# First attention of a two-layer block: values stationary and scaled probabilities moving, with the output made transposed in PSUM

## The reference, cut to what matters

```python
o_cmp = jnp.einsum('bghqc,bcgd->bqghd', p_cmp.astype(dt), vc_c)
...
o_slc = jnp.einsum('bghqk,bgqkd->bqghd', p_s.astype(dt), vs_g)
...
o_win = jnp.einsum('bghql,blgd->bqghd', p_w.astype(dt), vwin)
g = lax.dynamic_slice_in_dim(gate_a, q0, Q_BLOCK, axis=1)
o_a = g[..., 0:1] * o_cmp + g[..., 1:2] * o_slc + g[..., 2:3] * o_win
...
p_b = e / (e.sum(axis=-1, keepdims=True) + jnp.exp(sink - m))
o_b = jnp.einsum('bghql,blgd->bqghd', p_b.astype(dt), vbw)
return jnp.concatenate([o_a.reshape(B, Q_BLOCK, NSA_Q_W), o_b.reshape(B, Q_BLOCK, SWA_Q_W)], axis=-1)
```

## Time and profile before

| what | value |
|---|---|
| median of three runs | 3062.44 us (3058.03 to 3063.49) |
| the profiled execution's own time | 3059.4 us |
| its span | 3057.6 us |
| DMA share in the page's slices from 76 to 306 us | 0.3 |
| one weight load of 1 MB, issue to landing (median) | 4.8 us |
| ScalarE busy over the span | 1538.2 us (50%) |
| VectorE busy over the span | 2028.6 us (66%) |

### The profile page before, as it was taken

The page is one execution under the profiler, slowest core; times in us unless marked ns, Lnnn a source line. Parts: engine busy times, 40 slices in busy tenths (PEclk is TensorE's granted clock), DMA queues, the critical chain, the costliest instruction groups (busy, mean ns, idle before and its releaser), DMA issues.

```text
span 3057.6 us, 45171 instructions
## 1 busy us (share of the span) xinstructions
PE 3019.4 (99%) x16816; PEld 2615.9 (86%) x16816; DVE 2028.6 (66%) x2694; ACT 1538.2 (50%) x2134; POOL 20.6 (1%) x42
## 2 busy tenths in 40 slices
PE   9998999999999999999999999999999999999999
PEld 8997898888888888888888888888889888888887
DVE  5566679976888875555555555776566777777443
ACT  4554534555666665444444444544555555555333
POOL 2000000000000000000000000000000000000000
PEclk9999999999999999999999999999999999999999
DMA  7333545565566568766666666444455555555554
GB/s 269 133 132 116 188 159 196 204 228 187 186 239 240 213 219 296 249 240 242 242 241 241 241 241 233 163 147 163 152 179 179 181 195 187 191 180 192 196 189 179
DMA packets 138979, 615.20 MB, mean 201 GB/s; under 512 B 12989, under 2 KB 50062, under 8 KB 73968
## 3 DMA queue, kind: packets, MB, share of 16 engines
q1 hardware_dynamic: 126976, 583.05, 54.0%
q10 hardware_dynamic: 9440, 21.93, 2.0%
q0 software_dynamic: 2464, 8.89, 0.9%
HBM read 578.13 MB, written 36.49 MB: 201 GB/s over the span
## 4 chain that ended last, share of the span: by engine, by line
PE 76%; ACT 6%; DVE 5%; issue 3%; DMA 3%; ACTq 0%; DVEq 0%; SPq 0%
PE bank L642 75%; DMA raw<-in_experts_u_t 3%; ACT high L2275 3%; DVE low L1296 3%; ACT first_both L2520 1%; DVE first L1810 1%; ACT big L2528 1%; ACT big L2499 0%; ACT big L2493 0%; PE bank L912 0%; PE bank L732 0%; DMA raw<-in_w_down_t 0%; DVE resid L1928 0%; DVE big L1722 0%; ACT big L2307 0%
## 5 line engine op out<-in xcount | busy, mean ns | idle before, releaser
L1296 DVE TENSOR_TENSOR low<-raw,high 128x1024 fp32r<-128x1024 f32 x1008 | 1225.4, 1223 | 823.4 <-ACT high L2275 819.0
L2275 ACT ACTIVATE high<-raw 128x1024 fp32r<-128x1024 f32 x1008 | 1055.3, 1057 | 1064.9 <-PE bank L642 733.8
L642 PE MATMUL bank<-act_both,high 128*128 128x512 f32 (+1 forms) x5088 | 1169.2, 358 | 7.3 <-DVE low L1296 3.3
L642 PEld LDWEIGHTS bank<-act_both,high 128*128 128x128 f32 x5088 | 875.8, 190 | 123.5 <-issue 7.5
L642 PE MATMUL bank<-act_both,low 128*128 128x256 f32 x4240 | 713.3, 282 | 0.0
L642 PEld LDWEIGHTS bank<-act_both,low 128*128 128x128 f32 x4240 | 625.9, 191 | 33.1
L642 PE MATMUL bank<-high,weighed_high 128*128 128x512 f32 x1024 | 398.5, 389 | 0.0
L642 PE MATMUL bank<-high,weighed_low 128*128 128x512 f32 x1024 | 398.4, 389 | 0.0
L642 PE MATMUL bank<-low,weighed_high 128*128 128x512 f32 x1024 | 398.3, 389 | 0.0
L642 PE MATMUL bank<-high,act_both 128*128 128x512 f32 (+1 forms) x960 | 310.4, 393 | 3.6 <-DVE act_both L1358 3.6
L642 PEld LDWEIGHTS bank<-high,weighed_high 128*128 128x128 f32 x1024 | 192.3, 188 | 39.8
(11 more groups left out here) (286 smaller groups left out, 1923.1 us busy)
## 6 DMA issues: line engine op xcount, KB each, us to landing
raw<-in_experts_u_t SPq DMA_DIRECT2D x128, 1024.0 KB, 4.9
raw<-in_experts_v_t SPq DMA_DIRECT2D x128, 1024.0 KB, 4.8
raw<-in_w_up_t SPq DMA_DIRECT2D x88, 1024.0 KB, 4.8
raw<-in_w_in_t SPq DMA_DIRECT2D x68, 1024.0 KB, 4.8
raw<-in_w_down_t SPq DMA_DIRECT2D x44, 1024.0 KB, 4.8
raw<-in_w_out_t SPq DMA_DIRECT2D x32, 1024.0 KB, 4.8
raw<-in_peer_wq_t SPq DMA_DIRECT2D x16, 1024.0 KB, 4.8
hidden_dram<-big SPq DMA_DIRECT2D x64, 256.0 KB, 2.9
```

Of the source, the lines that this page charges most:

```text
L642: return pe.matmul(out_, lhs_t, rhs, start=start, stop=stop, skip_group_check=True)
L1296: dve.tensor_tensor(low[b][:, :], raw[r][:, HALF * which:HALF * (which + 1)], as_f32(high[b][:, :]), ALU.subtract).then_inc(low_ready[b], 1)
L2275: act.activation(high[b][:, :], raw[r][:, HALF * which:HALF * (which + 1)], ACT.Copy).then_inc(high_ready[b], 1)
```

## The change

`o1` becomes transposed: 16 chunks of 128 rows (two heads of 64, one from each group) by 256 tokens. In the mix, the values (64 columns) are stationary and the turned probabilities (128 or 256 columns) move; the two units of a pair write partitions 0 to 63 and 64 to 127 of the same bank. The branches of a head are summed in PSUM, so each branch's share, gate over sum, has to be in the probabilities before: VectorE computes it per pair (`shares_of`), and ScalarE multiplies the probabilities by it in four copies (`scale_probs`) before TensorE turns them. ScalarE copies finished banks to `o1` (`copy_chunks`). With `o1` transposed, `turn_o1` and the gain pass go, and the split into high and low parts is done on pairs of chunks. The compressed branch is computed in two parts, with pairs 4 and 20 (scores) and 8 and 24 (turning), and its mixes, now 16 products with 64 stationary columns, follow pairs 12, 14, 28 and 30. The slots change: turning moves from slot s+3 to s+4 and stands ahead of that slot's scores, mixing from s+4 to s+5, the copy of the transposes from s+2 to s+4 on ScalarE, and scaling has ScalarE's slot s+3. Rows of `w_out` are reordered on the host to match. In the diff below, the edits of compressed scores and tables are left out; they keep their amount of work.

```diff
-        o1 = r1.take(TT * D, "p (i d) -> p i d", i=TT)
+        o1_place = r1.take(TT * D)
+        o1 = o1_place.rearrange("p (c t) -> p c t", t=T)
+        attention_squares = o1_place.rearrange("p (i d) -> p i d", i=TT)
...
-        CMP_SCORES_WITH = {NSA_UNITS // 2 + 2 * i: i for i in range(TT)}
-        CMP_PROBS_WITH = {NSA_UNITS - 4 + 2 * g: g for g in range(2)}
+                h=c, swa=swa, g=g, branch=branch, part=part_no, col=SET * (2 * double + g) + j, j=j,
+                round=double - 2 if swa else double // 2))
+        CMP_SCORES_WITH = {4 + 16 * part: part for part in range(2)}
+        CMP_PROBS_WITH = {8 + 16 * part: part for part in range(2)}
...
             def attention_turn(n):
-                pe.wait_ge(probs_ready, 2 * (n + 2))
+                pe.wait_ge(probs_scaled, n + 2)
                 pe.wait_ge(probs_copied, n)
                 for g in range(2):
-                    for k, at in enumerate((0, P, T + 1)):
+                    for k, at in enumerate((T + 1, 0, P)):
                         m = pe.transpose(bank[:, 4 + g, P * k:P * k + P], logits1[:, (n + g) % LOGITS1, at:at + P], ident[:, :])
...
+            def chunk_at(j, g, first=0):
+                return bank[DH * g:DH * g + DH, 6 + j // 2, T * (j % 2) + first:T * (j % 2) + T]
             def attention_mix(n):
+                u = units1[n]
+                j, fresh = u["j"], u["branch"] != 1 and u["j"] % 2 == 0
                 pe.wait_ge(probs_copied, n + 2)
-                for u in units1[n:n + 2]:
-                    pt, o, at = probs_t1[:, u["g"], :], 6 + u["turn"] % 2, u["at"]
-                    if u["first"] and u["turn"] >= 2:
-                        pe.wait_ge(set_read, u["turn"] - 1)
-                    mm(bank[:, o, T + at:T + at + DH], pt[:, 0:P], u["v"][0], stop=False)
-                    mm(bank[:, o, T + at:T + at + DH], pt[:, P:T], u["v"][1], start=False)
-                    mm(bank[:, o, at:at + DH], pt[:, T:T + P], u["v"][0]).then_inc(mixed, 1)
+                if fresh and u["round"]:
+                    pe.wait_ge(chunks_copied, 2 * (u["round"] - 1) + j // 2 + 1)
+                for g in range(2):
+                    mm(chunk_at(j, g, P), units1[n + g]["v"][1], probs_t1[:, g, T:T + P], start=fresh, stop=False)
+                for g in range(2):
+                    m = mm(chunk_at(j, g), units1[n + g]["v"][0], probs_t1[:, g, 0:T], start=False, stop=u["swa"])
+                m.then_inc(mixed, 2)
+                if u["branch"] == 1 and j >= 2:
+                    pe.wait_ge(cmp_copied, u["part"] + 1)
+                    for c in (2 * j - 4, 2 * j - 3):
+                        for g in range(2):
+                            m = mm(chunk_at(c, g), cmp_v[:, SET * g + c, :], cmp_probs_t[:, u["part"], :], start=False)
+                    m.then_inc(chunks_done, 1)
...
+                if slot - 4 in pair_at:
+                    attention_turn(pair_at[slot - 4])
                 if slot in pair_at:
                     attention_scores(pair_at[slot])
-                if slot - 3 in pair_at:
-                    attention_turn(pair_at[slot - 3])
-                if slot - 4 in pair_at:
-                    attention_mix(pair_at[slot - 4])
-                if 43 <= slot < 47:
-                    cmp_mix(slot - 43)
...
+                if slot - 5 in pair_at:
+                    attention_mix(pair_at[slot - 5])
...
-            def turn_o1(half_):
-                for n in range(4):
-                    i, quarter = n // 2, 2 * half_ + n % 2
-                    if n == 0 and half_:
-                        pe.wait_ge(set_read, UNITS // SET + 4)
-                    elif n == 0:
-                        pe.wait_ge(o1_written, 4 + 4)
-                    if n >= 2:
-                        pe.wait_ge(turned_read, TURN0[1] + 4 * half_ + n - 1)
-                    for j in range(4):
-                        c = 4 * quarter + j
-                        m = pe.transpose(bank[:, 4 * half_ + n % 2, P * j:P * j + P], o1[:, i, P * c:P * c + P], ident[:, :])
-                    m.then_inc(turned, 1)
...
-            attention_slot(WOVEN)
-            attention_slot(WOVEN + 1)
-            turn_o1(0)
-            attention_slot(WOVEN + 2)
-            pe.wait_ge(turned_parts, PARTS0[1] + 4)
-            out_group(0, after=lambda k: attention_slot(WOVEN + 3 + k))
+            for slot in range(WOVEN, WOVEN + 3):
+                attention_slot(slot)
+            out_group(0, after=lambda k: attention_slot(WOVEN + 3 + k),
+                      before=lambda p: pe.wait_ge(turned_parts, PARTS0[1] + p + 1))
             pe.wait_ge(logits_ready, 2 * UNITS)
-            out_group(1)
-            turn_o1(1)
+            out_group(1, after=lambda k: attention_slot(WOVEN + 3 + QUAD + k))
             out_group(2)
             out_group(3)
...
+            def split_o1(*pairs_):
+                for n in pairs_:
+                    two = slice(2 * n, 2 * n + 2)
+                    dve.wait_ge(turned_high, PARTS0[1] + n + 1)
+                    dve.tensor_tensor(act_low[:, two, :], o1[:, two, :], as_f32(act_high[:, two, :]), ALU.subtract).then_inc(turned_parts, 1)
...
-            def attention_set(n):
...
+            def shares_of(n):
...
+                heads = slice(u["h"], u["h"] + GROUP_HEADS + 1, GROUP_HEADS)
+                dve.wait_ge(probs_ready, 2 * (n + 2))
+                sums = expsum1.rearrange("p (i n) -> p i n", i=TT)[:, :, u["col"]:u["col"] + SET + 1:SET]
+                m = dve.reciprocal(sums, sums)
+                if not u["swa"]:
                     dve.wait_ge(small_copied, 1)
-                    link(dve.tensor_tensor(sums, sums, gate1[:, :, heads, 1 + branch], ALU.mult))
-                at = N * (g + 2 * (branch == 2)) + DH * SET * part_no
-                part_ = o1[:, :, at:at + DH * SET].rearrange("p i (h d) -> p i h d", d=DH)
-                dst = share1.rearrange("p (i h d) -> p i h d", i=TT, d=DH) if branch == 1 else part_
-                m = dve.tensor_tensor(dst, bank[:, 6 + turn_ % 2, :].rearrange("p (i h d) -> p i h d", i=TT, d=DH),
-                                      row(sums, DH), ALU.mult)
-                m.then_inc(set_read, 1)
-                dve.wait_ge(set_read, turn_ + 1)
-                if branch == 1:
-                    add_o1(part_, dst)
...
+                    link(m)
+                    m = dve.tensor_tensor(sums, sums, gate1[:, :, heads, 1 + u["branch"]], ALU.mult)
+                m.then_inc(shares_ready, 2)
...
             def attention_slot(slot):
-                if slot - 5 in pair_at and units1[pair_at[slot - 5]]["last"]:
-                    for g in range(2):
-                        attention_set(pair_at[slot - 5] + g)
+                if slot - 2 in pair_at:
+                    shares_of(pair_at[slot - 2])
                 if slot in pair_at:
                     attention_logits(pair_at[slot])
-                if slot == 19:
-                    cmp_logits_done()
-                elif slot == 27:
-                    cmp_probs_done()
-                elif 44 <= slot < 48:
-                    cmp_set(slot - 44)
+                if slot % 16 == 5 and slot < 32:
+                    cmp_logits_done(slot // 16)
+                elif slot % 16 == 9 and slot < 32:
+                    cmp_probs_done(slot // 16)
...
+            split_o1(0, 1)
             attention_slot(WOVEN)
+            split_o1(2, 3)
             attention_slot(WOVEN + 1)
-            split_o1(0)
+            split_o1(4, 5)
             attention_slot(WOVEN + 2)
...
+            def scale_probs(n):
+                act.wait_ge(shares_ready, n + 2)
+                for u in units1[n:n + 2]:
+                    at_ = logits1[:, (n + u["g"]) % LOGITS1, :]
+                    for at, width, col in ((0, T, UNITS + u["col"]), (T + 1, P, u["col"])):
+                        m = act.activation(at_[:, at:at + width], at_[:, at:at + width], ACT.Copy, scale=expsum1[:, col:col + 1])
+                m.then_inc(probs_scaled, 2)
...
+            def copy_chunks(n):
+                if n < 4:
+                    act.wait_ge(chunks_done, n + 1)
+                else:
+                    act.wait_ge(mixed, NSA_UNITS + 4 * (n - 3))
+                act.activation(o1[:, 2 * n:2 * n + 2, :].rearrange("p c t -> p (c t)"), bank[:, 6 + n % 2, :], ACT.Copy).then_inc(chunks_copied, 1)
+            chunks_at = {18: 0, 20: 1, 34: 2, 36: 3, 40: 4, 44: 5, 56: 6, 60: 7}
             def attention_slot(slot):
-                if slot - 2 in pair_at:
-                    copy_probs1(pair_at[slot - 2])
+                if slot in chunks_at:
+                    copy_chunks(chunks_at[slot])
+                if slot - 4 in pair_at:
+                    copy_probs1(pair_at[slot - 4])
                 if slot in pair_at:
                     exps1(pair_at[slot])
-                if slot == 25:
-                    act.wait_ge(cmp_shifted, 1)
```

(51 more changed lines are left out.)

141 lines of the change are left out of this document (37 added, 104 removed).

## The result

The changed kernel takes **3089.8 us** (median of 6 runs, 3086.9 to 3092.2), the kernel before 3061.8 on the same chip: ratio 1.0093, 95% interval 1.0080 to 1.0106, so slower. The forecast was 3082 (3068 to 3092). The profiled execution spans 3088.9 us against 3057.6, 31.3 more where the sum said 20.

What follows compares the result with a forecast made beforehand. TensorE bounded the kernel before; the change was to make it wait on a 7.0 us ring. Window terms +20.2, -2.8, -6.6, +11.2, -2.2 sum to about +20: 3079.4, with 3.0 for the median 3082 us, range 3068 to 3092.

Steps and rivals of the forecast that it cites:

- The ring: Woven attention pairs: scores, maxima, exponentials, scaling, turn, next scores form a closed loop of 7.0 us; TensorE stands 1.4 us a pair.
- 0.58 of turning: Last work link of the loop: TensorE's transposes of a pair's probabilities, priced at 0.58 us from the earlier trace.
- the first term: Second pair's scores to pair 38's: 132.4 us against 112.25, +20.2, of which 18 x 7.0 = 126.0.
- the clock falls in the stalls: Rival: TensorE's stops through 18 woven pairs bring it to 1.2 GHz, 75 us more, about 3157; chance 0.03.
- The two compressed score sets: Woven stretch: two compressed score sets on the loop, 36 against 20 instructions, 2.11 us each.
- The group changes: Woven stretch: two changes of product group, where query copies hold TensorE, 0.5 us each.
- sinks and compressed logits: Woven stretch: charged 1.2 us together within the window from second pair's scores to pair 38's.
- Mix: TensorE's mix, eight instructions a pair: 0.96 us, 0.29 less than now; bounds 0.68 side by side, 1.36 one after the other.
- the rival of serial column groups: Rival: column groups run one after the other, mixes cost 1.36 to 1.66, hidden: 3085; counted within the forecast's 0.82.
- To the output product: Input product's end to output product: 4.7 us against 11.29, -6.6, as turn_o1(0), its gains and a 3.63 us wait go.
- Output group 0: 33.9 us against 22.72, +11.2: an 8.7 us stop at pair 40's turn, two loops of 8.0, slow clock 1.4.
- The ring that never binds: Rival: scaling does not stand behind the next exponentials, TensorE stays the bound; about -17 us, 3046; chance 0.09.

Runs made afterwards that it cites:

- run 1: Changed kernel with ScalarE scaling pair s-2 at the head of slot s, before the copy of turned probabilities and the exponentials: 3060.0 us.
- run 2: Changed kernel with three useless scaled copies added on ScalarE ahead of the four real ones of each pair: 3116.5 us.
- run 3: Changed kernel without the four scaling copies of each pair; the turn waits for the exponentials instead: 3050.4 us.
- run 4: Changed kernel with TensorE issuing the scores of pair s before the turn of pair s-4, ScalarE's order unchanged: 3072.7 us.
- run 7: Changed kernel with useless identity transposes on TensorE only in long stops (first turn, group changes, input product's end): 3084.5 us.
- run 6: Changed kernel with twelve useless identity transposes on TensorE ahead of every turn's wait for the scaling: 3092.2 us.
- run 8: Changed kernel with ScalarE's slot ordered copy of pair s-3, scaling of s-2, exponentials of s, and later splits of output chunks: 3049.3 us.
- run 9: Changed kernel with copy, scaling, exponentials in that order, later chunk splits, and two turns moved ahead of the query copies: 3048.0 us.
- run 5: Changed kernel with scaling at the head of ScalarE's slot for pairs 0 to 38 alone, later pairs as changed: 3062.5 us.

## Why the prediction was right, point by point

**The ring** was right in its mechanism and in every link but the turn (scores to maxima 3.11, exponentials 1.77, scaling 1.48), and shown by undoing it (run 1), lengthening it (run 2), taking it away (run 3) and shortening it at another place (run 4). Its prices held too: the 256-wide scaled copy took 494 ns (499 taken), the 128-wide one 388 (391).

**Mis-sized: the turn's link.** "0.58 of turning" came from the earlier trace rows, where the input product follows. In the changed kernel scores follow, and the same six transposes take 0.81. Run 1 has both in one trace: 0.57 ahead of the product, 0.75 ahead of scores. The ring is 7.25 us instead of 7.0, and 18 x 0.25 is 4.5 of the 11.6 us that the first term lacks. The forecast did cite the Trainium skill, TensorEngine Tiling (Array Packing), section Tiling Modes, on the drain at a change of tiling mode, but weighed it for the mix alone; the trace agrees with it here, at 0.18 us.

**Mis-sized: the clock.** The rival "the clock falls in the stalls" was refused for the whole, at +75 us, and rightly: the ring's own stops of 1.5 us leave the granted clock at 1.00 from 128.68 to 157.90. The waits that bring the low clock back each time, of which the Trainium skill tells (TensorE: Matmul & The Clock Gate, section HAM oscillation), are not what these rows show for the ring. The page's waits, put there at some 3 to 5 us, are also longer than the ring's, so "by that rule this would be the outcome" did not follow from it. But the margin was small: with 1 us more on the ring the granted clock of the stretch fell to 0.87 (run 2). And it came true in places, after the stop of 3.5 us at the first turn and after some of the stops of about 2, and the fillers put a price on that: 4.7 us in the woven stretch, of 11.6. The forecast charged a low clock only in the output group.

The other 2.4 us (11.6 - 4.5 - 4.7) lie in run 7's trace as follows. 1.3 is low clock that was left there: behind the stop of 1.87 score groups start 10.33 and 7.98 us apart, where run 6, at full clock, has 9.75 and 7.25. The two compressed score sets cost 0.4 each more than charged (9.75 instead of 7.25 + 2.11), and the first ring takes 7.88, 0.6 more than the others. The group changes come to the 0.5 each that was charged (7.77), and sinks and compressed logits to 0.4 less than charged. So by these traces the clock cost 6.0 us in all, the largest part of the 11.6.

**Mix.** 0.80 us (131.15 to 131.95) instead of 0.96, between the bounds and near the 0.68 of two abreast; the rival of serial column groups (1.36 and up) is out. It lies beside the ring's wait and earned nothing while the ring is closed.

**To the output product,** 5.13 for 4.7: the second scores came at the low clock (1.65 us for 0.92). **Output group 0,** 34.61 for 33.9, right in the sum and different inside. TensorE's timeline there:

```profile
274.71 1.65 PE L645 MATMUL bank<-big 64*128 64x256 f32 x8 [1.29 <-DVE big L1417]
...
287.20 1.54 PE L915 MATMUL bank<-turn_consts,big 128*128 128x128 f32 x6 [5.85 <-ACT big L2286]
...
296.88 0.87 PE L915 MATMUL bank<-turn_consts,big 128*128 128x128 f32 x6 [2.29 <-ACT big L2286]
...
305.85 0.88 PE L915 MATMUL bank<-turn_consts,big 128*128 128x128 f32 x6 [1.68 <-ACT big L2286]
```

Pair 40's turn begins 16.0 us after the input product's end (271.16), as ScalarE's order said (16.2); the stop ahead of it is 5.85, not 8.7, since TensorE had reached it late, at the low clock. In run 7, where fillers kept the clock up, the same stop is 8.63. A low clock ahead of a fixed appointment costs nothing. Behind the stop it was paid: the two rings took 9.7 and 9.0 for 8.0, 2.1 of it turns and scores at the low clock (1.54 for 0.88 and twice 1.6 for 0.92), where the forecast had 1.4 for a clock that comes back slowly; the rest is mostly the turn's link again. The stops at the end of these two rings are 2.29 and 1.68, where the forecast said two near 2.7.

**The ring that never binds,** the rival on the other side, was priced at 3046, some 17 us under the kernel before. Runs 8 and 9 come nearest to that kernel: 3049.3 and 3048.0, 11.6 and 12.9 us under it as timed beside them; run 3, without scaling, is 9.4 under. Up to the input product's end run 9 has the gains as sized (110.29 and 18.43 us, where the rival's terms make 110.45 and 18.88). From there to the end of output group 1 it takes 41.55 us, where they make 37.4: TensorE waits 4.0 us there for ScalarE's copies, which the rival's sum does not have.

**The range** held, with 3089.8 near its upper end, and that is luck in part. The text works out 3070 to 3092 and gives 3068 to 3092; its upper end was made of a dearer scaled copy, a dearer mix, a longer stop at pair 40 and 2 us of clock. The copy, the mix and the stop came out at or under their prices, and the excess came from the turn's link, which had no margin, and from three times the 2 us of clock.

## What to carry to other kernels

A step added between two engines is priced by the loop that it closes, not by the engine's slack: follow one item through every engine's program order until it comes back to where it began, and compare that time with the busiest engine's work per item. If the loop is longer, look first for an order that opens it; here one moved line on ScalarE gave back the whole loss, and further moves turned it into a gain. A stop on TensorE can have a second price, the low clock after it, but only where what follows is not waiting for something else anyway. Look also at what follows a borrowed row: six transposes cost more ahead of scores than ahead of the product that the row had.

## What the runs showed of the hardware

- The same six transposes take 0.57 us ahead of products with 128 stationary rows and 0.75 ahead of products with 64 (run 1; 0.81 after a stop, changed kernel): a change of tile adds about 0.18 us.
- Two column groups of 64 run side by side: the mix's eight instructions (384 moving columns for each group) take 0.80 us, where one group after the other would take 1.36 by the compress products of the earlier trace rows.
- Repeated stops of 1.48 us every 7.25 left the granted clock at 1.00 (128.68 to 157.90); the same ring with nine stops of over 2 us in it ran at 0.87 (run 2). One stop of 3.5 us was followed by 12.6 us at 0.56.
- A stop of about 2 us can go either way. In the changed kernel the stop of 2.15 us before 163.39 is followed by the low clock, the equal one before 226.71 is not, and in run 6 the first of the two is not and the second is:

```profile
163.39 0.51 PE L645 MATMUL bank<-act_both,high 128*128 128x256 f32 x2 [2.15 <-DVE big L1577]
...
165.15 1.48 PE L915 MATMUL bank<-turn_consts,big 128*128 128x128 f32 x6
...
226.71 0.50 PE L645 MATMUL bank<-act_both,high 128*128 128x256 f32 x2 [2.15 <-DVE big L1577]
...
228.24 0.82 PE L915 MATMUL bank<-turn_consts,big 128*128 128x128 f32 x6
```

- Of the fourteen unfilled stops of 2.1 to 2.4 us at a change of group in the changed kernel and in runs 1, 3, 4, 5, 6 and 8, ten are followed by some 10 us at 0.82 to 0.87 and four by 1.00. What decides is not shown.
- With transposes of an identity matrix in the first stop the granted clock stayed at 1.00 (107.84 to 125.48 in run 7, also 106.03 to 123.64 in run 6, where 1.76 us of the stop remained); without them it fell to 0.68 (107.09 to 128.68).
